# Two blocks in one launch: VectorE sums the squares behind the gated embedding, and the last stage scales six early tiles before the late half's last addition

## The reference

```python
# end of the first block
h = h + jax.nn.sigmoid(h @ w_ple_gate[i]) * (p[i] @ w_ple_proj[i])
# head of the second block
def rmsnorm(x, g):
    y = xf * lax.rsqrt(jnp.mean(xf * xf, axis=-1, keepdims=True) + EPS)
    return (y * g.astype(jnp.float32)).astype(x.dtype)
h = rmsnorm(x, ln_attn_pre[l])
mix = token_mixer(h, w_in[l], ...)      # its first step is proj = h @ w_in
# last line of the second block
x = x + rmsnorm(u @ w_down[l], ln_mlp_post[l])
```

## Time and profile before

| | |
|---|---|
| median of 3 runs | 1319.65 us (1318.61 to 1320.53) |
| the profiled execution, its time | 1317.35 us |
| its span, first to last instruction | 1315.1 us |
| TensorE busy | 1281.4 us (97%) |
| VectorE busy | 771.3 us (59%) |
| ScalarE busy | 551.3 us (42%) |
| GpSimd busy | 43.4 us (3%) |
| mean granted clock of TensorE | 0.995 |

### The profile page before, as it was taken

The page is one execution under the profiler, slowest core; times in us unless marked ns, Lnnn a source line. Parts: engine busy times, 40 slices in busy tenths (PEclk is TensorE's granted clock), DMA queues, the critical chain, the costliest instruction groups (busy, mean ns, idle before and its releaser), DMA issues.

```text
span 1315.1 us, 17501 instructions
## 1 busy us (share of the span) xinstructions
PE 1281.4 (97%) x6418; PEld 1078.4 (82%) x6418; DVE 771.3 (59%) x1241; ACT 551.3 (42%) x913; POOL 43.4 (3%) x45
## 2 busy tenths in 40 slices
PE   9999999999999999999989999999999999999997
PEld 7887887998888888888868888787997888888886
DVE  7876686466444443333774886798867522355334
ACT  5656675343222223322553654567543222222221
POOL 3000000000000000000030000000000000000002
PEclk9999999999999999999989999999999999999998
DMA  5232113122222333323233322423112322233322
GB/s 194 82 98 77 33 33 109 53 63 83 97 97 96 101 97 120 110 98 112 84 108 89 105 81 81 120 73 113 49 49 81 110 96 96 81 97 96 111 96 80
DMA packets 37067, 119.91 MB, mean 91 GB/s; under 512 B 4492, under 2 KB 6668, under 8 KB 37008
## 3 DMA queue, kind: packets, MB, share of 16 engines
q1 hardware_dynamic: 35744, 116.93, 27.8%
q0 software_dynamic: 544, 1.58, 0.4%
q10 hardware_dynamic: 720, 0.60, 0.1%
HBM read 111.74 MB, written 2.11 MB: 87 GB/s over the span
## 4 chain that ended last, share of the span: by engine, by line
PE 81%; DVE 13%; ACT 4%; issue 2%; DMA 0%; SPq 0%; ACTq 0%; DVEq 0%
PE bank L903 25%; PE bank L905 25%; PE bank L904 25%; DVE w_lo L2146 3%; DVE tiles L2146 2%; DVE tiles L2149 1%; PE bank L1004 1%; DVE arena L2146 1%; ACT w_hi L1547 1%; DVE negmax L2366 1%; DVE probsT L2146 1%; PE bank L1097 1%; DVE arena L2149 1%; DVE residual L2146 1%; PE bank L1429 1%
## 5 line engine op out<-in xcount | busy, mean ns | idle before, releaser
L2146 DVE TENSOR_TENSOR w_lo<-raw_slab,w_hi 128x1024 fp32r<-128x1024 f32 x198 | 244.9, 1237 | 280.0 <-ACT w_hi L1547 278.9
L903 PE MATMUL bank<-u_hi,w_hi 128*128 128x512 f32 x824 | 324.8, 394 | 6.6 <-DVE w_lo L2146 2.8
L905 PE MATMUL bank<-u_hi,w_lo 128*128 128x512 f32 x824 | 321.9, 391 | 0.0
L904 PE MATMUL bank<-u_lo,w_hi 128*128 128x512 f32 x824 | 321.9, 391 | 0.0
L1547 ACT ACTIVATE w_hi<-raw_slab 128x1024 fp32r<-128x1024 f32 x198 | 208.7, 1054 | 181.6 <-PE bank L905 177.1
L903 PE MATMUL bank<-arena,w_hi 128*128 128x512 f32 (+1 forms) x692 | 261.3, 378 | 2.1 <-DVE w_lo L2146 1.1
L904 PE MATMUL bank<-arena,w_hi 128*128 128x512 f32 (+1 forms) x692 | 259.3, 375 | 0.0
L905 PE MATMUL bank<-arena,w_lo 128*128 128x512 f32 (+1 forms) x692 | 259.2, 375 | 0.0
L903 PEld LDWEIGHTS bank<-u_hi,w_hi 128*128 128x128 f32 x824 | 155.2, 188 | 41.3 <-DVE w_lo L2146 4.5
L905 PEld LDWEIGHTS bank<-u_hi,w_lo 128*128 128x128 f32 x824 | 155.2, 188 | 33.0
L904 PEld LDWEIGHTS bank<-u_lo,w_hi 128*128 128x128 f32 x824 | 155.4, 189 | 30.4
(11 more groups left out here) (270 smaller groups left out, 1481.9 us busy)
## 6 DMA issues: line engine op xcount, KB each, us to landing
raw_slab<-in_stream SPq DMA_DIRECT2D x198, 512.0 KB, 3.4
aside_raw<-in_stream SPq DMA_DIRECT2D x8, 512.0 KB, 5.7
arena<-arena SPq DMA_DIRECT2D x32, 128.0 KB, 2.3
residual<-in_xT SPq DMA_DIRECT2D x8, 256.0 KB, 6.6
out_hT<-residual SPq DMA_DIRECT2D x12, 128.0 KB, 1.7
arena<-forget_rows SPq DMA_DIRECT2D x8, 128.0 KB, 2.3
tiles<-in_pT POOLq DMA_DIRECT2D x2, 256.0 KB, 3.1
tiles<-bias_rows POOLq DMA_DIRECT2D x1, 512.0 KB, 4.8
```

The lines of the kernel that those rows point to most:

```text
L903: pe.matmul(o, ws[0], xs[0], start=first, stop=False)
L904: pe.matmul(o, ws[0], xs[1], start=False, stop=False)
L905: return pe.matmul(o, ws[1], xs[0], start=False, stop=last)
L2146: return nc.vector.tensor_tensor(o, a, b, op)
```

## The change

VectorE runs the seven additions of squares of `pre_2` in place of GpSimd, one behind `next_lo(4)`, one behind `ple(6)`, one behind `ple(7)` and four behind the `w_lo` of dk0. `stat` stands one k later in dk0. GpSimd still waits for the sum before its bias load. In the last stage VectorE scales tiles 3, 4 and 5 of the early half (and adds tile 3) before `last_sum(1, LATE)`, and takes the late half's reciprocal after all early tiles.

```diff
--- before.py
+++ after.py
@@ -860,11 +860,6 @@
             for k in range(2):
                 pool.dma_start(t(TMP + k), pT_in[k * P:(k + 1) * P, :]).then_inc(sem.p_loaded, 16)
 
-            for k in range(1, KD):
-                pool.wait_ge(sem.sq_done, SQ0["pre_2"] + k + 1)
-                if k > 1:
-                    pool.wait_ge(sem.ssum_done, ADD0["pre_2"] + k - 1)
-                nc.gpsimd.tensor_tensor(t(PROB), t(PROB), t(k), ALU.add).then_inc(sem.ssum_done, 1)
             pool.wait_ge(sem.ssum_done, ADD0["pre_2"] + ADDS["pre_2"])
             skewed = bass.AP(tensor=scratch.tensor, offset=scratch.offset, ap=[[1, P], [S, DF_H], [1, BIAS_W]])
             pool.dma_start(tiles[:, MO:MO + DF_H, 0:BIAS_W], skewed).then_inc(sem.bias_loaded, 16)
@@ -1370,7 +1365,7 @@
                         places[k]("pre_2")
 
             first_projection("dq0", True, {})
-            first_projection("dk0", False, {3: stat, KD - 1: spread})
+            first_projection("dk0", False, {4: stat, KD - 1: spread})
             tokens("dv", "dv")
             projection("dq1")
 
@@ -2202,9 +2197,9 @@
                 dve.wait_ge(sem.ssum_done, ADD0[name] + n + (not name.endswith("_b")))
                 tt(tiles[:, SSUM, part_], tiles[:, SSUM, part_], tiles[:, SQ + m % 2, part_], ALU.add).then_inc(sem.ssum_done, 1)
 
-            def add_all(name):
-
-                for k in range(1, KD):
+            def add_all(name, first=1, end=KD):
+
+                for k in range(first, end):
                     dve.wait_ge(sem.sq_done, SQ0[name] + k + 1)
                     if k > 1:
                         dve.wait_ge(sem.ssum_done, ADD0[name] + k - 1)
@@ -2751,13 +2746,17 @@
             slab_lo(SLAB0["ple"] + 6)
             ple(5)
             next_lo(4)
+            add_all("pre_2", 1, 2)
             next_lo(5)
             slab_lo(SLAB0["ple"] + 7)
             ple(6)
+            add_all("pre_2", 2, 3)
             next_lo(6)
             ple(7)
+            add_all("pre_2", 3, 4)
             next_lo(7)
             slab_lo(SLAB0["dq0"])
+            add_all("pre_2", 4)
             slab_lo(SLAB0["dk0"])
             inverse_root("pre_2")
             have_factors(3)
@@ -2994,13 +2993,13 @@
             for c, (name, part_) in enumerate((("mlp_post_2", EARLY), ("mlp_post_2_b", LATE))):
                 factor = rstd(name)
                 for k in range(KD):
-                    if c == 0 and k == 3:
+                    if c == 0 and k == 6:
                         last_sum(1, LATE)
                     stt(tiles[:, k, part_], tiles[:, k, part_], col("ln_mlp_post_2", k), factor[:, part_], ALU.mult, ALU.mult).then_inc(sem.y_scaled, 1)
                     if k not in BY_POOL[name]:
                         dve.wait_ge(sem.y_scaled, Y0[name] + k + 1)
                         tt(h_sb[:, k, part_], h_sb[:, k, part_], tiles[:, k, part_], ALU.add).then_inc(sem.h_done, 1)
-                    if c == 0 and k == KD - 3:
+                    if c == 0 and k == KD - 1:
                         inverse_root("mlp_post_2_b")
```

## The result

| | before | changed |
|---|---|---|
| median of 6 runs | 1319.43 us (1317.94 to 1320.53) | 1309.96 us (1307.57 to 1311.67) |
| ratio, 95% interval | | 0.9928 (0.9915 to 0.9941) |
| profiled execution: time, span | 1317.35, 1315.1 us | 1309.69, 1307.9 us |

The kernel is 9.5 us faster by the medians, 7.8 to 11.2 us by the interval. The forecast was 1311.0 us, 8.6 us faster. One run of the last kernel in the table of experiments took 1355.32 us at a mean granted clock of 0.906, its other five had 0.995 to 0.998; it is left out of that kernel's interval.

A forecast was written before the change was run, and what follows sets the result against it. TensorE, busy 97% of the span, was taken to bound the kernel, with waits and a slow clock at 668 to 694 us. Gains of 8.1 + 0.5 = 8.6 us from 1319.65 gave 1311.0 us, range 1309.0 to 1315.0 (8 in 10).

The forecast's parts named there:

- What bounds: Hand-over from gated embedding to second block's norm: TensorE waits 2.3 us for w_lo, 1.79 for u_lo, then runs at 1.2 GHz.
- The stretch is GpSimd's: At 652 to 684.5 us, GpSimd's additions of squares lengthen VectorE's w_lo, products and u_lo by 6.4 us in all.
- rival (c): Slower: the stretch belongs to the stage itself and lengthens VectorE's new additions to 1.77 us; 1322.5 us, chance 0.03.
- The chain from T: From T, start of the last gate product's last matmul (673.69 us): dk0's w_lo ends at T + 5.00, wanted at T + 5.67.
- The sum of part 1: Moving seven pre_2 additions to VectorE shortens 668.25 us to the spread from 25.52 to 17.45 us: 8.1 us gained.
- The last four additions: Behind dk0's w_lo, from 678.6 to near 681.5 us; statistics matmul 1.3 us after their sum, bias load about 2 us earlier.
- Part 2: Last stage: three scalings move into VectorE's idle time, late tiles start 0.64 us earlier; 0.5 us taken, given GpSimd's additions.
- The sum of both: Whole kernel: 8.1 us from the moved additions plus 0.5 us from the last stage, 8.6 us gained.
- rival (a): A gap stays before dk0 or the u_lo and the clock stays low: only about 4 to 5 us back, 1315.2 us, chance 0.13.

The follow-up runs named there:

- the last kernel in the table of experiments: The changed kernel with GpSimd's seven additions for the first norm (attn_pre) moved to VectorE too: 1309.69 us, ratio to before 0.9930.
- the two kernels with idle GpSimd work: The changed kernel plus seven unused GpSimd instructions at the old places: additions 1314.38 us (0.9966 to before), or fills that read no tile 1309.83 us (0.9925).
- part 1 alone: The changed kernel with the last stage put back, so only the seven additions move to VectorE: 1312.05 us, ratio to before 0.9941.
- the two kernels with additions in front: The changed kernel with four, or two, of the last four additions put before the w_lo of dk0: 1313.13 us (0.9955 to before) and 1310.01 us (0.9930).
- part 2 alone: The kernel before with only the last stage changed: 1318.00 us, ratio to before 0.9992.
- the kernel with the old place: The changed kernel with the statistics matmul back behind 12 matmuls of dk0: 1310.66 us, ratio to before 0.9930.
- four additions in front: The changed kernel with the last four additions before the w_lo of dk0 instead of behind it: 1313.13 us, ratio to before 0.9955.
- two additions in front: The changed kernel with two of the last four additions before the w_lo of dk0 and two behind: 1310.01 us, ratio to before 0.9930.

## Why the prediction was right

1. **What bounds**, TensorE's waits and the clock behind them at 668 to 694 us: shown, by their absence in the changed kernel and by 8.03 us less distance, and by the return of 2.9 us of waits and 3.86 us of distance when GpSimd adds again.
2. **The stretch is GpSimd's.** Shown by the two kernels with idle GpSimd work: additions bring it back and fills do not. That it is their reading is the likeliest account, as said there. The forecast said 6.4 us of stretch; now 6 w_lo and 8 u_lo take 7.3 + 6.0 us where they took 8.7 + 8.1, and 8 products at 687 ns are 2.9 us below 8.4: 6.4 us. VectorE's own additions take 687 ns in the mean as well, where rival (c) needed over 1.4 us. The rule of the Trainium skill (SBUF — State Buffer, Who interferes with whom) is about every VectorE instruction with two inputs in SBUF, the tile memory; the trace agrees, since the products and the w_lo were stretched as well as the u_lo. By the same section of the Trainium skill a GpSimd instruction that only writes does not contend with them; the trace agrees, with a u_lo of 0.75 us beside a fill of 0.96. The Trainium skill (Perfetto Trace Analysis, Optimizing Scalar/DVE Operations) says that giving work of a saturated VectorE to GpSimd may make sense, and adds that between these two it might not help. The kernel before does give this work to GpSimd and is 7.8 us slower than part 1 alone, so the reservation is what held.
3. **The chain from T.** In the changed trace T is 675.28 us, or 673.70 without the 1.58 us by which that execution was late; the forecast was 673.69. The sigmoid of tile 7 starts at 675.70, T + 0.42 and not T + 0.26: I had read the start of a piece of the chain (652.10) as that of a matmul, and that matmul had started 0.17 us before:

```profile
651.93 0.39 PE L905 MATMUL bank<-arena,w_lo 128*128 128x512 f32 x1
```

The w_lo of dk0 ends 4.74 us behind the sigmoid, to the hundredth as forecast (5.00 - 0.26), so at T + 5.16, where TensorE wants it at T + 5.67. That leaves 0.51 us, and the two kernels with additions in front measured 0.45, as a matmul that waits starts some 0.05 us behind its w_lo. It was forecast as 0.6 (5.67 - 5.00 is 0.67, rounded down); it held. The spread stands at T + 12.04, forecast T + 12.0.

4. **The sum of part 1**, 8.1 us: 8.03 in the traces, 7.8 (5.9 to 9.5) in the times. That it agrees to 0.1 us in the traces is in part luck. It was worked out from one execution of the kernel before, in which the clock stayed low for long; against the one of part 2 alone, with the same waits, part 1 is worth 40.06 - 33.38 = 6.7 us.
5. **The last four additions** end at T + 8.15 where T + 7.8 was reckoned: 0.16 from the chain, the rest because they start 0.80 us apart ((3.08 - 0.69) / 3), not 0.73. The statistics at T + 9.07 have 0.9 us of room instead of 1.3. The bias load goes out 1.5 us earlier (683.72 less the 1.58, against 683.61), where about 2 was forecast. Nothing hung on either, as the kernel with the old place shows for the statistics.
6. **Part 2**: 0.64 forecast for the late tiles' start, 0.63 measured; 0.5 after GpSimd's interference, 0.68 measured. The interference that I subtracted was there (0.58 and 0.66 us for the early additions of 0.42), but it fell into room: the reciprocal starts at 1300.03, 0.04 us behind the end of the root, as in the kernel before. Of the 0.3 us of room that I saw there, 0.24 was used.
7. **The sum of both**, 8.03 + 0.68 = 8.7 us, is what the traces show from these two places. The spans differ by only 7.2 us, because the profiled execution of the changed kernel lost 1.5 us elsewhere. GpSimd's timeline dates it; changed kernel, then before:

```profile
125.61 0.52 POOL L857 DMA_DIRECT2D bias_rows<-tiles  x1 [101.59 <-DVE tiles L2502]
500.97 1.11 POOL L861 DMA_DIRECT2D tiles<-in_pT  x2 [374.83 <-DVE tiles L2141]
```

```profile
125.55 0.52 POOL L857 DMA_DIRECT2D bias_rows<-tiles  x1 [101.60 <-DVE tiles L2507]
499.39 1.10 POOL L861 DMA_DIRECT2D tiles<-in_pT  x2 [373.31 <-DVE tiles L2146]
```

Between 126 and 500 us the changed kernel's execution falls back by 1.5 us, in code that the change does not touch. The stretches around 204 us, changed kernel and then before:

```profile
200.00:204.00 4.00, 2.04 (x12) 1.49 (x12) 3.93 (x9) 1.36 (x4) 0.00 (x0) 1.00 0.37 73
204.00:209.00 5.00, 5.00 (x24) 4.58 (x24) 2.58 (x8) 1.05 (x3) 0.00 (x0) 0.66 0.90 361
```

```profile
200.00:204.00 4.00, 2.05 (x13) 1.49 (x12) 3.93 (x9) 1.36 (x4) 0.00 (x0) 1.00 0.23 60
204.00:209.00 5.00, 5.00 (x33) 4.35 (x32) 3.11 (x9) 2.03 (x5) 0.00 (x0) 1.00 0.93 374
```

Up to 204 us both are alike; then one execution ran at 0.66 of the clock and the other at 1.00. That accounts for the 1.5 us by place. It is not the change: GpSimd's idle time between the two loads is 373.3 to 373.4 us in four of the ten traces (before, part 1 alone, part 2 alone, four additions in front), with the granted clock at 1.00 from 204 to 209 us, and 374.8 to 374.9 us in the other six, with 0.66 to 0.75. The medians, 9.5 us apart, lie 0.8 us above the 8.7, inside their interval.

What was off: the price of rival (a). I gave 3.0 us (2.6 for twelve matmuls and 0.4 for the statistics) for a clock that stays low behind gaps of about a microsecond, and 1.0 for the gaps. With two additions in front, a gap of 0.78 us cost 1.08 us of distance in all. Gaps of 0.78, 2.38, and 1.53 with 1.02 us left it at 1.00 in these executions.

## What to carry to other kernels

An idle GpSimd is not free help beside a VectorE that sets the pace: before giving it an addition, look for VectorE instructions with two inputs in the tile memory that start with it or in it and last longer than their peers. Moving the work back costs its 0.7 us per tile only where no wait of VectorE covers it, so write the chain of the stage from one event and put the moved instructions into its holes; here 0.45 us of slack decided where four of them could stand. In a last stage, work moved into an idle gap returns no more than the distance to the next thing that the end waits for: 0.6 of 1.7 us here.

## What the runs showed of the hardware

- A GpSimd addition holds a VectorE instruction up, and a fill does not. An addition of two different tiles of 512 columns held a VectorE instruction with two inputs up for 1.1 us (1.84 against 0.74), a tile added to itself for 0.8 us (1.58), a fill of 1024 columns not at all (0.75). Both delays are 0.19 us less than the GpSimd addition took (1.29 and 1.03). VectorE's scalings whose second input lies in PSUM kept starting 0.39 to 0.40 us apart beside GpSimd's additions in the last stage, while the additions to the residual took up to 0.66 instead of 0.42 us. It goes both ways: behind a w_lo that had started 0.30 us before it, GpSimd's second addition took 2.05 us.

```profile
660.65 1.21 DVE L2146 TENSOR_TENSOR w_lo<-raw_slab,w_hi 128x1024 fp32r<-128x1024 f32 x1
660.95 2.05 POOL L867 TENSOR_TENSOR tiles<-tiles 128x512 f32<-128x512 f32 x1 [0.79 <-ACT tiles L1929]
```

- Dependent additions of 512 columns on VectorE start 0.80 us apart in a row of four, a product and a sum 0.73 us.
- The granted clock behind the same waits differs between executions. At 204 us, after waits of 0.9, 1.3 and 2.0 us that agree to 0.02 us, it was 1.00 in one profile and 0.66 in another; the difference was 1.5 us of the kernel's time. Behind gaps of 1.8 and 1.2 us before dk0 the slow stretch took in twelve matmuls and the statistics in one execution and about seven matmuls in another, 1.35 us less in all. What decides it was not tried. The 1.5 us alone are over a third of the spread of the runs of one kernel (1307.57 to 1311.67 us).
